# Built gates copied and multiplied tile by tile with four tokens inside, and what stands around them in order

## The reference, cut to what matters

```python
y = jnp.concatenate([y_mix, y_mem], axis=-1) * jax.nn.silu(gate)      # first block
...
v1, i1 = lax.top_k(s[:, :, 0], K)                                     # peer_ffn, K = 16
v2, i2 = lax.top_k(s[:, :, 1], K)
top_s, pos = lax.top_k(cand, K)
g = jax.nn.softmax(top_s, axis=-1)
a = jnp.einsum('thkd,td->thk', ue, xb)      # ue: the chosen rows of u
w = jax.nn.gelu(a) * gb
return jnp.einsum('thk,thkd->td', w, ve)    # ve: the chosen rows of v
...
g_ple = jax.nn.sigmoid(rmsnorm(x, norm_ple[i]) @ ple_gate[i])         # second block, end
x = x + g_ple * (p[i] @ ple_proj[i])
```

## Time and profile before

| What | us |
| --- | --- |
| median of 3 executions (lowest to highest) | 3073.13 (3072.13 to 3076.7) |
| the profiled execution, its own time | 3074.83 |
| its span, from the first to the last instruction | 3072.7 |
| PE busy | 2788.7 (91%) |
| DVE busy | 1863.5 (61%) |
| ACT busy | 776.8 (25%) |
| POOL busy | 733.1 (24%) |

### The profile page before, as it was taken

The page is one execution under the profiler, slowest core; times in us unless marked ns, Lnnn a source line. Parts: engine busy times, 40 slices in busy tenths (PEclk is TensorE's granted clock), DMA queues, the critical chain, the costliest instruction groups (busy, mean ns, idle before and its releaser), DMA issues. The chain is left out here.

```text
span 3072.7 us, 28611 instructions
## 1 busy us (share of the span) xinstructions
PE 2788.7 (91%) x9498; PEld 1611.8 (52%) x9498; DVE 1863.5 (61%) x3615; ACT 776.8 (25%) x2034; POOL 733.1 (24%) x601
## 2 busy tenths in 40 slices
PE   9999999999888989998899988999988899988955
PEld 4454435454554444445655677878777544433422
DVE  4998622008774232347742667999667777657784
ACT  1114310102331011344531231212444311112122
POOL 0530000000000000002210355444100255545672
PEclk9999999999999989999999999999999999999977
DMA  5221112212001221110022599998544599999993
GB/s 192 78 86 55 69 73 91 82 55 82 29 28 41 82 85 56 58 55 28 28 89 94 207 382 378 343 320 319 209 131 132 188 409 409 409 412 390 398 375 138
DMA packets 125763, 544.44 MB, mean 177 GB/s; under 512 B 13888, under 2 KB 14272, under 8 KB 117568
## 3 DMA queue, kind: packets, MB, share of 16 engines
q0 software_dynamic: 73728, 268.47, 23.1%
q1 hardware_dynamic: 49472, 258.02, 22.5%
q10 hardware_dynamic: 2432, 16.29, 1.4%
HBM read 538.52 MB, written 4.19 MB: 177 GB/s over the span
## 5 line engine op out<-in xcount | busy, mean ns | idle before, releaser
L1142 PE MATMUL ps<-XTD,STREAM 128*128 128x256 f32 x2048 | 461.6, 384 | 21.9 <-ACT GD L1641 13.5
L1170 PE MATMUL ps<-STREAM,GD 128*128 128x512 f32 x1024 | 458.3, 604 | 23.0 <-DMA STREAM<-experts 17.8
L606 PE MATMUL ps<-XT,W 128*128 128x512 f32 (+1 forms) x1216 | 471.8, 548 | 6.9 <-issue 4.5
L1142 PEld LDWEIGHTS ps<-XTD,STREAM 128*128 128x128 f32 x2048 | 387.5, 192 | 82.3 <-DMA STREAM<-experts 16.5
L1801 POOL DMA_INDIRECT ROW_U<-peer_u,C x208 | 254.4, 1223 | 470.2 <-DVE DOT L2448 444.6
L606 PEld LDWEIGHTS ps<-XT,W 128*128 128x128 f32 x1216 | 229.6, 190 | 248.0 <-issue 238.4
L1170 PEld LDWEIGHTS ps<-STREAM,GD 128*128 128x128 f32 x1024 | 190.7, 192 | 288.7 <-issue 207.6
L2460 DVE SCALAR_TENSOR_TENSOR X<-ROW_V,WEIGHT,X 128x1024 f32<-128x1024 f32 x208 | 267.1, 1284 | 98.6 <-DMA ROW_V<-peer_v,C 82.3
L2448 DVE CUSTOM_DVE_ANT_0 ROW_U<-ROW_U,XN 128x1024 f32<-128x1024 f32 x208 | 253.8, 1220 | 62.9 <-DMA ROW_U<-peer_u,C 55.5
L1810 POOL DMA_INDIRECT ROW_V<-peer_v,C x208 | 234.2, 1126 | 155.6 <-DVE X L2460 119.1
L721 PE MATMUL ps<-W,Y 128*128 128x512 f32 x512 | 225.5, 601 | 13.1 <-DVE Y L1972 6.1
(11 more groups left out here) (347 smaller groups left out, 3827.8 us busy)
## 6 DMA issues: line engine op xcount, KB each, us to landing
STREAM<-experts SPq DMA_DIRECT2D x256, 512.0 KB
W<-wstream SPq DMA_DIRECT2D x53, 2048.0 KB, 8.4
GD<-wstream ACTq DMA_DIRECT2D x2, 2048.0 KB, 15.7
ROW_U<-peer_u,C POOLq DMA_INDIRECT x208
ROW_V<-peer_v,C POOLq DMA_INDIRECT x208
XT<-xT SPq DMA_DIRECT2D x8, 256.0 KB, 5.3
W<-wstream SPq DMA_DIRECT2D x8, 256.0 KB, 5.8
X<-x SPq DMA_DIRECT2D x1, 2048.0 KB, 19.5
```

What stands on the lines that cost most here:

```text
L606: mm = pe.matmul(b[:, 0:rhs[k].shape[-1]], w[:, k, m * P:(m + 1) * P], rhs[k], start=(k == 0), stop=(k == KD - 1))
L1142: mm = pe.matmul(UP_BANK[g % 2][:, 0:256], u[:, k, :], XTD[:, k, :], start=(k == 0), stop=(k == KD - 1))
L1170: mm = pe.matmul(acc(b, n)[:, :], GD[:, i * 256 + b * P:i * 256 + (b + 1) * P], STREAM[m % STREAM_RING][:, n * T:(n + 1) * T], start=(i == ...
```

## The change

Six things are edited together.

1. `keep_quad` and `quad_gates` walk over tiles in the outer loop and the four tokens of the quad in the inner one. The same elements are read and written. In `GD` four neighbouring elements (16 bytes) are now touched one after the other, then a step of 1 KB; in the PSUM bank each element lies 512 bytes behind the one before it. Before, it was steps of 1 KB in `GD` and neighbours in PSUM.
2. `ones_ahead(g)`: those quads of the next step whose buffer is free are written and scaled at the start of a step; rows stand between `tile_gates` and `quad_gates`.
3. `rows_by` gives one row for every two steps in the quad phase: 117 rows at step 127, so 139 remain.
4. The picks are spread otherwise over the rows (`routed_by_row`), and forced later.
5. In stage b `silu` is (1 + tanh(x/2)) * x, with the factor 0.5 taken in at the output: one DVE instruction where there were three.
6. The last layer: both blocks 2 and 3 are prepared in the last rows, and the projection of block 1 is done before the last row.

```diff
+def ones_ahead(g):
+
+    free = quads_by(g - 1) + 2
+    return [q for q in quads_of(g + 1) if q < free], [q for q in quads_of(g + 1) if q >= free]
+
+
...
-    return rows_by(QUAD_FROM) + (g - QUAD_FROM) // 4
+    return rows_by(QUAD_FROM) + (g - QUAD_FROM) // 2
...
+def routed_by_row(r):
+
+    first, due = rows_by(TILES - 1), UNITS // 2 * UNIT_ROWS - 4
+    steps = ROUTE_STEPS + 1
+    return 12 * ROUTE_STEPS + 6 + (steps * (r - first + 1) // (due - first) if r < due
+                                   else steps + steps * (r - due + 1) // UNIT_ROWS)
...
-        DENSE = GD[:, :].rearrange("p (i t) -> p t i", i=TILES)
+        DENSE = GD[:, :].rearrange("p (i t) -> p i t", i=TILES)
...
-        PLE_T = ((2, 3), (2, 3), (2, 3), (4, 5))
-        PLE_S = ((0, 1), (0, 1), (0, 1), (6, 7))
+        PLE_T = ((2, 3), (2, 3), (4, 5), (2, 3))
+        PLE_S = ((0, 1), (0, 1), (6, 7), (0, 1))
+        PLE_J = ((2, 3), (2, 3), (4, 5), (6, 7))
...
-                if i in (100, 101):
-                    ple_gates(0, i - 100)
-                if i == 103:
+                if i in (102, 103):
+                    ple_gates(0, i - 102)
+                if i == 105:
                     ple_proj(0)
-            for i in range(1, 4):
-                ple_transposes(i)
+            ple_transposes(1)
+            ple_transposes(2)
+            for i in (1, 2):
                 ple_gates(i, 0)
                 ple_gates(i, 1)
                 ple_proj(i)
+            ple_proj(3)
+            ple_transposes(3)
+            ple_gates(3, 0)
+            ple_gates(3, 1)
...
-            def gate_exponential(j):
+            def gate_tanh(j):
                 act.wait_ge(gate_full, 16 + j + 1)
-                act.activation(gate_tile("b", j), FILL_BANK[j % 2][:, :], ACT.Exp, scale=-1.0).then_inc(gate_exp, 1)
+                act.activation(gate_tile("b", j), FILL_BANK[j % 2][:, :], ACT.Tanh, scale=0.5).then_inc(gate_half, 1)
...
-                act.activation(DENSE[:, 4 * q:4 * q + 4, g + 1:TILES],
-                               BUILD_BANK[q % 3][:, :].rearrange("p (t i) -> p t i", t=4)[:, :, g + 1:TILES], ACT.Copy
+                act.activation(DENSE[:, g + 1:TILES, 4 * q:4 * q + 4],
+                               BUILD_BANK[q % 3][:, :].rearrange("p (t i) -> p i t", t=4)[:, g + 1:TILES, :], ACT.Copy
...
+                ahead, behind = ones_ahead(g)
+                for q in ahead:
+                    scale_quad(q)
+                row_weights(rows_by(g) - LAG)
                 for q in quads_of(g):
                     keep_quad(q, g)
-                for q in quads_of(g + 1):
+                for q in behind:
                     scale_quad(q)
-                row_weights(rows_by(g) - LAG)
...
-                dve.wait_ge(gate_exp, j + 1)
-                dve.tensor_scalar(g, g, 1.0, None, ALU.add).then_inc(gate_part, 1)
-                dve.wait_ge(gate_part, 2 * j + 1)
-                dve.reciprocal(g, g).then_inc(gate_part, 1)
-                dve.wait_ge(gate_part, 2 * j + 2)
-                dve.tensor_tensor(g, g, FILL_BANK[j % 2][:, :], ALU.mult).then_inc(gate_done, 1)
+                dve.wait_ge(gate_half, j + 1)
+                dve.scalar_tensor_tensor(g, g, 1.0, FILL_BANK[j % 2][:, :], ALU.add, ALU.mult).then_inc(gate_done, 1)
...
-                    while routed < UNITS and 32 * routed - r <= 10:
+                    while routed < UNITS and 32 * routed - r <= 4:
...
-                view = DENSE[:, 4 * q:4 * q + 4, 0:g + 1]
-                dve.tensor_tensor(view, view, BUILD_BANK[q % 3][:, :].rearrange("p (t i) -> p t i", t=4)[:, :, 0:g + 1],
+                view = DENSE[:, 0:g + 1, 4 * q:4 * q + 4]
+                dve.tensor_tensor(view, view, BUILD_BANK[q % 3][:, :].rearrange("p (t i) -> p i t", t=4)[:, 0:g + 1, :],
...
+                ahead, behind = ones_ahead(g)
+                for q in ahead:
+                    quad_ones(q)
                 if gated(g) > 0:
                     tile_gates(g)
+                rows_to(rows_by(g))
                 for q in quads_of(g):
                     quad_gates(q, g)
-                for q in quads_of(g + 1):
+                for q in behind:
                     quad_ones(q)
-                rows_to(rows_by(g))
...
-                if r == ROWS - 20:
+                if r == ROWS - 17:
                     add_sums(2)
                     add_sums(3)
...
-            for i in (2, 3):
-                ple_scale(i)
-                ple_factor(i)
-            for i in (2, 3):
-                ple_out(i)
+            ple_out(2)
+            ple_scale(3)
+            ple_factor(3)
+            ple_out(3)
```

More of the change, by code:

```diff
@@ L1159, in build_quad @@
                 for i in range(4):
-                    mm = pe.matmul(BUILD_BANK[q % 3][:, i * P:(i + 1) * P], ONE[q % 2][:, 1, i, :], ONE[q % 2][:, 0, i, :],
-                                   start=True, stop=True)
+                    mm = pe.matmul(BUILD_BANK[q % 3][:, i * P:(i + 1) * P], ONE[q % 2][:, 1, i, :],
+                                   ONE[q % 2][:, 0, i, :], start=True, stop=True)
                 mm.then_inc(built, 1)
@@ L1179, in ple_transposes @@
                 b = PLE_ORDER[i]
[L1180 to L1181 removed]
+                if i in (1, 3):
+                    pe.wait_ge(y_ready, 2 if i == 1 else 4)
                 for half in range(2):
@@ L1296, in att_steps @@
                         if t == gate_step(stage, j) + 1:
-                            (gate_silu if stage == "a" else gate_exponential)(j)
+                            (gate_silu if stage == "a" else gate_tanh)(j)
             def out_projection(name, n, roots=1):
@@ L1733, in _ @@
                     act.dma_start(XB, x_kept).then_inc(x_back, 16)
-                if r == rows_by(TILES - 1) + 92:
+                if r == rows_by(TILES - 1) + 87:
                     ple_copies(0)
                     ple_roots(0)
-                if r == rows_by(TILES - 1) + 97:
+                if r == rows_by(TILES - 1) + 93:
                     ple_sigmoid(0)
+                if r == ROWS - 16:
+                    ple_copies(1)
+                    ple_copies(2)
                 if r == ROWS - 14:
-                    ple_copies(1)
                     ple_roots(1)
-                if r == ROWS - 8:
+                    ple_roots(2)
+                if r == ROWS - 9:
                     ple_sigmoid(1)
                 row_weights(r + 1)
-            for i in (2, 3):
-                ple_copies(i)
-                ple_roots(i)
-                ple_sigmoid(i)
+            ple_sigmoid(2)
+            ple_copies(3)
+            ple_roots(3)
+            ple_sigmoid(3)
         @block.gpsimd
@@ L1954, in att_steps @@
                             dve.wait_ge(bank_free, POS["gate_b"] + head + 1 + 4)
-                        dve.tensor_tensor(yt(y), OT_BANK[head % 2][:, :], gt(y), ALU.mult).then_inc(at_y, 1)
+                        if stage == "b" and head >= 4:
+                            dve.scalar_tensor_tensor(yt(y), OT_BANK[head % 2][:, :], 0.5, gt(y), ALU.mult, ALU.mult
+                                                     ).then_inc(at_y, 1)
+                        else:
+                            dve.tensor_tensor(yt(y), OT_BANK[head % 2][:, :], gt(y), ALU.mult).then_inc(at_y, 1)
             att_steps("a")
@@ L2549, in ple_out @@
                     dve.wait_ge(ple_proj_full, 2 * i + n + 1)
-                    ch.link(dve.tensor_tensor(gate, gate, ps[PLE_T[i][n]][:, :], ALU.mult))
+                    ch.link(dve.tensor_tensor(gate, gate, ps[PLE_J[i][n]][:, :], ALU.mult))
                     dve.tensor_tensor(xb(b)[:, cols], xb(b)[:, cols], gate, ALU.add).then_inc(y_ready, 1)
```

27 lines of the change are left out of this document (16 added, 11 removed).

## The result

| What | Before | After |
| --- | --- | --- |
| median us (lowest to highest, 4 executions each) | 3073.68 (3072.13 to 3076.7) | 2963.5 (2960.15 to 2967.83) |
| profiled execution, own time; span | 3074.83; 3072.7 | 2962.04; 2959.9 |

The two profiled executions divide as follows. The quad phase is counted from the end of the first build to the end of the last, read off in order of time.

The account below looks back on a forecast made before the run. No engine was taken to bound the whole: gate waits, a quad-phase loop through DVE, DMA from 2480 us, and PE's tail. Terms -22 + 0 - 1 - 27 - 19.5 = -69.5 from 3073.1 gave 3004 us; range 2990 to 3016, with rivals 2986 to 3034.

Parts of the forecast that it names:

- Term 1: Stage b's attention: the shorter gate work on DVE removes PE's waits for the copied tile, -22 us (ends -10 and -28).
- Term 2: Quad phase, multiply and copy: with the new walk a mean multiply takes 0.62 us, upper bound 1.1 us.
- the first rival: PSUM read in steps keeps the quad-phase multiply at 1.1 us: +17 us, 3021 us in all, chance 0.2.
- Term 3: Quad phase with new order and 11 more rows: steps sum to 257.8 us against 257.3 before, so 0.
- Term 4: Behind the quad phase, where DMA is full: 11 rows fewer at 2.565 us each, -27 us (ends -33 and -15).
- Terms of the ends: Last multiplies of the quad phase end about 1 us sooner, -1; less work behind the last row, -19.5 us.
- the cover: Last rows: time to spare, 17 us, for blocks 2 and 3 to have their products done by the last row.
- the low ends given for the terms: Most favourable values: -28 us for stage b's gates, -10 for the quad phase, -33 for the rows behind it.
- The rivals: Whole-kernel cases: 3021 us (chance 0.2), about 3024 (0.17), 3015 (0.1), slower than before (0.03), no effect (0.01).
- The chance of faster: Whole kernel: 0.95 that the change makes it faster, against 0.02 for the same and 0.03 for slower.

Follow-up runs that it names:

- eighth run: The changed kernel with no row in the quad phase and 161 rows behind it: 3011.41 us, ratio 0.98.
- Run 5: The changed kernel with the old walk of the multiply and the copy, everything else as changed: 2995.21 us, ratio 0.9745.
- 4: The kernel before with only the walk of the multiply and the copy turned round: 3050.25 us, ratio 0.9917.
- run 7: The changed kernel with one row for every four steps of the quad phase, 11 there and 150 behind: 2983.8 us, ratio 0.9693.
- run 6: The changed kernel with the old order within a quad-phase step on DVE and ACT, keeping 22 rows and the new walk: 2969.71 us, ratio 0.9648.
- run 8: The same run as the eighth run: the changed kernel with no row in the quad phase, 3011.41 us, ratio 0.98.

## Why the prediction was wrong

**Term 1, the gates (-22; measured -35.3 to the first build, -33.5 with this part alone).** The mechanism was right: the reciprocal goes, and every wait of L703 with it. The size was off. The prediction's "PE is what is left as the bound, and where the clock fell after such waits a little more may come back. I take -22" counted the waits and added 1.5. The waits were 20.5 of it; 3.5 more was the wait for the last output tile, which hangs on the same list of DVE, and 8.9 was busy time of the same matmuls, some 5 of it by the lower clock. That makes 32.9; 1.8 us of the 35.3 lie ahead of the attention and 0.6 behind it, where nothing was changed.

**Term 2, the multiply (0.62 us; measured 0.589).** Right, and the first rival (1.1 us) fell with it. By the sentence of the Trainium skill cited in the prediction ("Advanced Engine Details and Errata", Memory Cachelines) steps in PSUM might have been dear. For a reader on DVE with steps of 512 bytes the trace says no: 0.97 ns for an element, as for neighbours. What such steps would do to matmuls, of which the page speaks, no run here shows.

**Term 3, the quad phase (0; measured -25.2).** This is the step that failed, and it begins with the first sentence: "The floor of a step is PE: 3.43 us for a tile's products (8 x 2 passes, 3.62 with the last one's fill) plus 1.16 for each build". Those rows are of builds that had waited for one-hot rows. Without a wait the groups follow each other closer. The eighth run shows the floor: 4.35 us with one build and 5.24 with two, so about 3.45 for the products, near the 3.43 taken, but 0.9 for a build, not 1.16.

| Step (with a row in the step before) | Count | Forecast | Measured | Sum of difference |
| --- | --- | --- | --- | --- |
| one after two | 8 | 4.7 | 4.57 | -1.0 |
| one after two (row) | 10 | 7.1 | 6.05 | -10.5 |
| two after one | 11 | 5.8 | 5.24 | -6.2 |
| two after one (row) | 8 | 6.65 | 5.86 | -6.3 |
| one after one | 7 | 4.6 | 4.35 | -1.8 |

The differences add up to -25.8; the sum in the prediction, 257.8, less the measured 232.1 is 25.7. The largest part, 10.5 us, is the one-quad step with a row. Its sum used a second number from the same stalled place, that `tile_gates` ends 0.52 us before the builds; it ends 1.06 before, which is about half of the difference. The two-quad step with a row stood at 6.65 without its working, so only its measured 5.86 can be told. The 0 was itself made of two errors on one side. With the old price of the multiply the prediction's sum is 275: it gave order and rows +18 us (275 against 257.3) and the walk -17 (257.8 against 275). Run 5, with order and rows but the old walk, took 263.4, which is +6, and the walk then gives 31.3. So "What the order gains they use up" holds to within 3 to 6 us, and the walk's gain comes on top. One way to add up the runs is the walk 28.3 (4), the order 9.5 (4 and 7), eleven more rows 12.6 (7 and the changed kernel): 257.3 - 28.3 - 9.5 + 12.6 = 232.1. Over run 6 the same sum has 6.2 for the rows and 3.1 for the order.

**Term 4, eleven rows fewer (-27; measured -31.6).** Within its ends. Eleven rows more cost R 33.8 us in run 7 and 22 more cost 64.5 in run 8, so 2.9 to 3.1 for a row, where 2.565 was taken. That price was worked out at 409 GB/s, and the stretch has parts below it. Which of them a row lengthens wasn't tried; with R's scatter of 5 us, the 4.6 by which the term was missed can't be divided further.

**Terms of the ends (-1 and -19.5; measured -1.6 and -19.1).** Right. Block 3's products were done 22.6 us before the last row's end, where the cover was put at 17; but the projection of block 1, which waits for block 3's sigmoid, leaves PE only 6.6 us to spare.

**The range.** Term 3 alone would have given 3004 - 25 = 2979, already under the 2986 of the range. Even the low ends given for the terms (6 us more for the gates, 10 for the phase, 6 for the rows) add up to 2982: the range had no room for two terms that miss on the same side.

**The rivals.** None came true. The cases listed all lay above the forecast, and the one that happened, more gain in two terms at once, wasn't among them. Its only traces were the end of -28 for the gates and "Fewer stalls than summed, because rows drift, would give -10". The chance of faster was right.

## What to carry to other kernels

Take the floor of a step from rows in which the engine did not wait, and from start to start: a group that begins after a wait, or a group's end, includes time that disappears in a full pipeline. When a wait on TensorE goes, look also for a lower granted clock behind it and for every other wait on the same late list; here the waits named were 20.5 us of a gain of 33. Before moving work into a cheaper stretch, try where in the step it costs least: the same 25 small pieces of work cost 20.7 us (232.9 against 212.2) in one place and 44.2 in another.

## What the runs showed of the hardware

An f32 multiply on DVE costs 2.13 ns for an element when its SBUF side goes in steps of 1 KB, and 0.97 when it touches four neighbours at a time, though PSUM is then read in steps of 512 bytes. ACT's copy with the same two walks fell from a mean of 324 to 239 ns. A reciprocal of 128x512 takes 3353 ns on DVE and one of 128x256 takes 1753, while an add and multiply in one takes 681 for 128x512.
